# S5 outputs of two state tiles at a time, alternating between column groups of the matmul array

## Chip, cores and metric

The kernel runs on one core of a Trainium2 chip. The metric is the device time of one execution in microseconds (us). Beside the times there is one profiled execution, from which all rows of the trace come. TensorE does the matmuls (PE in the rows, PEld its weight loads), VectorE is DVE, ScalarE ACT, GpSimd POOL, SyncE SP.

## What is computed

Two layers of a decoder trunk over 512 positions and 2048 channels. Each layer projects the modulated input to four branches of 512 channels, which are gated, joined and projected back. Cut to the branch that the change is about:

```python
for l in range(DEPTH):
    h = x * (1.0 + scale) + shift
    proj = h @ w_in[l]                       # (512, 2048) @ (2048, 6144)
    y_a = gated short convolution            # a_b, a_c, a_x, a_g
    y_b = dilated attention * silu(b_g)      # q, k, v, b_g
    y_c = rglru_branch(c_x, ...) * silu(c_g)
    y_d = s5_branch(d_u, ...) * silu(d_g)
    y = concatenate([y_a, y_b, y_c, y_d]) @ w_out[l]
    x = layer_norm(ALPHA * x + (1.0 + gate) * y)

# S5: 32 groups of 16 channels, each with 64 complex diagonal states
bu = ug @ bb                                 # "drive" of the states, complex
x_re, x_im = scan(x = a * x_before + bu)     # along the positions
y = c_re . x_re - c_im . x_im + d_skip * u   # "output"
y = gelu(y); y = y * sigmoid(y @ w_glu + b_glu)
```

## The kernel before

Each layer has a branch loop of four steps (`Fori(0, CT)`), and a step makes 128 channels of every branch. The input projection is cut into 12 units of 128 channels (`UNITS`), each unit into two halves, so a step has `HALF` = 24 slots (n = 0 to 23). A slot is 24 matmuls of 128x512 in fp32r: eight with `op_hi` and eight with `op_lo` on the weights' high part, eight with `op_hi` on their low part (L915, L916, L922). All other TensorE work of a step stands behind a slot: `put(n, part)` appends a part to slot n, and TensorE does parts and slots strictly in that order. The parts that matter here:

- `s5_drive(q)`, q = 0 to 3 (slots 5, 7, 10, 13; L807): the drive of state tile q, 128 of the step's 512 complex states, into banks 2 and 3.
- `s5_output(q)` (slots 9, 12, 16, 19; L813, L814): two fp32 matmuls, with the real and the imaginary states (`s5_s[3]`, `s5_s[4]`) as moving tiles of 128x512, into the 32 partitions of bank 4 that begin at 32q, so in column group q of the array. It waits for `x_rot`, which VectorE raises at the end of `s5_out(q)`, and raises `c_done`.
- `scores(t)` (slots 9, 10, 12, 13; L835), attention scores for two heads; `p_turn(g)` (slots 16, 18, 20; L849), transposes of the probabilities, head 0 and then head 1. `p_turn(0)` waits for `p_norm` head by head. `weigh(g)` (slots 18, 20, 22; L861) multiplies probabilities and values, the two heads in two halves of the array's columns. An fp32 matmul shows as two instructions.

The outputs wait on a chain of VectorE, whose order is also written out by hand (`branch_loop`): `s5_in(q)` turns the drive, `s5_scan(q)` scans it, `s5_out(q)` turns the result back into `x_re`, `x_im` (six instructions of 128x512). All four tiles use the same five tiles `s5_s`, so `s5_out(q)` waits for `c_done` of output q - 1. Between them stand `ada` pieces (two at a time in layer 0, one in layer 1), the RG-LRU, `score_max(t)`, which waits for `scores(t)`, and `normalise(h)`, which raises `p_norm`. The part of the order around tile 2, before:

```python
score_max(3); s5_scan(2); ada(2, 1)
s5_out(2); normalise(0); ada(2, 1); normalise(1)
own(silu2(0, "c_g", gx[:, 0, :]), s.own)
dve.wait_ge(x_io.sem, 16 * (1 + (ST if l else 0)))
own(stt(y_out(2), xc, 0.5, gx[:, 0, :], MUL, MUL), s.gate_used[0])
s5_in(3); s5_scan(3); ada(2, 1); s5_out(3)
```

`own` issues an instruction and waits for its end. ScalarE (ACT) splits weights, copies units out of their banks, writes the gates' tanh and copy into `gt` and `gx` (`gate`), and copies transposed probabilities (`p_copy`) into `p_t`.

Of the kernel before, what the change touches and what calls it, by code (L numbers as in the profile page):

```python
# [31 lines left out]
ST = S // P  # L32
# [5 lines left out]
SQ = 4  # L38
# [77 lines left out]
def trunk(nc, A, out):  # L116
# [5 lines left out]
    with ExitStack() as ctx:  # L122
# [19 lines left out]
        s5_w = sb("s5_w", [P, 4, P])  # L142
# [28 lines left out]
        u_d, xc, q_t, k_t, v_t = (work[:, i, :] for i in range(5))  # L171
        u_swap = work[:, 17, :]
        s5_s = [work[:, 5 + i, :] for i in range(5)]
# [7 lines left out]
        p_t = [(work[:, 14, :], work[:, 15, :]), (q_t, k_t)]  # L181
        gx = work[:, 16:18, :]
        gt = work[:, 18:20, :]
        silu_d = work[:, 20:24, :]
        ax = xp[:, 3:3 + S]
        gel = s5_s[3]
        gate_b = work[:, 0:4, :]
        scale_acc = [ada_acc[:, 0, :], ada_acc[:, 1, :], ada_acc[:, 2, :], work[:, 20, :]]
        glu_t = work[:, 14:18, :]
# [23 lines left out]
        bank = [ctx.enter_context(nc.psum_tensor(f"bank{i}", [P, S], F32)) for i in range(8)]  # L213
# [15 lines left out]
        x_io = signal("x_io")  # L229
# [8 lines left out]
        for l in range(DEPTH):  # L238
            s, n = Layer(), f"_{l}"
# [308 lines left out]
        def _(act):  # L548
# [19 lines left out]
            for l, s in enumerate(layers):  # L568
# [26 lines left out]
                with act.Fori(0, CT) as ct:  # L595
# [10 lines left out]
                    def gate(name, i, use):  # L606
                        ps, free = unit(name)

                        act.wait_ge(s.gate_used[i].sem, s.gate_used[i].at(use, ct))
                        act.activation(gt[:, i, :], ps, ACT.Tanh, scale=0.5)  # L610
                        act.activation(gx[:, i, :], ps, ACT.Copy).then_inc(free.sem, 1)
# [9 lines left out]
                    def p_copy(g):  # L621
                        n = sum(P * (ST - kb) for kb in TURNS[g])
                        if g != 1:
                            act.wait_ge(s.pv_done.sem, s.pv_done.at(g, ct))
                        for h in range(2):
                            act.wait_ge(s.full[5 + h].sem, s.full[5 + h].at(1 + ST + g + 1, ct))
                            act.activation(p_t[h][g % 2][:, 0:n], bank[5 + h][:, 0:n], ACT.Copy).then_inc(s.p_copy.sem, 1)
# [23 lines left out]
                    for n in range(2, HALF):  # L651
                        split_hi(n, ct)
                        if n == 3:

                            act.wait_ge(s.free[4].sem, s.free[4].at(0, ct))
                            ps, free = unit("d_u")
                            act.wait_ge(s.gate_used[1].sem, s.gate_used[1].at(0, ct))
                            act.activation(u_d, ps, ACT.Copy)
                            for h in range(2):
                                swapped = act.activation(u_swap[64 * h:64 * h + 64, :], ps[64 - 64 * h:128 - 64 * h, :], ACT.Copy)  # L660
                            swapped.then_inc(free.sem, 1)
                        if n == 5:
                            act.wait_ge(s.step_end.sem, s.step_end.at(0, ct))
                            copy("c_x", xp[:, 3:3 + S])
                            rotation()
                        if n == 7:
                            copy("q", q_t, HD ** -0.5)
                        if n == 8:
                            lru()
                        if n == 9:  # L670
                            copy("k", k_t)
                        if n == 11:
                            copy("v", v_t)
                        if n == 13:
                            gate("c_g", 0, 0)
                        if n == 14:

                            act.wait_ge(s.full[7].sem, s.full[7].at(s.full[7].per, ct))
                            act.wait_ge(s.pv_done.sem, s.pv_done.at(0, ct))
                            act.activation(work[:, 10, :], bank[7][:, :], ACT.Copy).then_inc(s.free[7].sem, 1)  # L680
                        if n in (15, 16):
                            exps(n - 15)
                        if n == 15:
                            act.wait_ge(s.full[3].sem, s.full[3].at(SQ, ct))
                            gate("d_g", 1, 0)
                        if n in (18, 20, 22):
                            p_copy((n - 18) // 2)
                        if n == 17:
                            copy("a_c", va[:, 2:2 + S])
                        if n == 19:  # L690
                            copy("a_x", ax)
                        if n == 21:
                            gate("b_g", 0, 1)
                        if n == 23:
                            gate("a_g", 1, 1)
# [34 lines left out]
        def _(pe):  # L730
# [30 lines left out]
            for chunk in range(4):  # L761
                channels(layers[0], range(4 * chunk, 4 * chunk + 4))
                pe.wait_ge(pro_used.sem, KT * (chunk + 1))
                for j in range(8):
                    mm = pe.matmul(bank[7][:, j:j + 1], pro_acc[chunk % 2][:, j // 4, P * (j % 4):P * (j % 4 + 1)],
                                   ones[:, 0:1], start=True, stop=True)
                mm.then_inc(pro_sum.sem, 1)

            for l, s in enumerate(layers):
# [11 lines left out]
                with pe.Fori(0, CT) as ct:  # L781
# [25 lines left out]
                            fill(2 + i, pe.matmul(bank[2 + i][:, :], s5_w[row:row + 32, i, :], u[row:row + 32, :],  # L807
                                                  start=True, stop=True))

                    def s5_output(q):  # L810
                        pe.wait_ge(s.x_rot.sem, s.x_rot.at(q + 1, ct))
                        o = bank[4][32 * q:32 * q + 32, :]
                        pe.matmul(o, s5_w[:, 2, 32 * q:32 * q + 32], s5_s[3], start=True, stop=False)  # L813
                        mm = pe.matmul(o, s5_w[:, 3, 32 * q:32 * q + 32], s5_s[4], start=False, stop=True)  # L814
                        mm.then_inc(s.c_done.sem, 1)

                    def lru_gates():
                        pe.wait_ge(s.xc_done.sem, s.xc_done.at(1, ct))
# [70 lines left out]
                    def put(n, part, *args):  # L889
                        between[n].append(lambda: part(*args))  # L890

                    put(3, s5_turn)
                    put(6, lru_gates)
                    for q, (at_drive, at_output) in enumerate(((5, 9), (7, 12), (10, 16), (13, 19))):
                        put(at_drive, s5_drive, q)
                        put(at_output, s5_output, q)
                    for t, at in enumerate((9, 10, 12, 13)):
                        put(at, scores, t)
                    put(11, v_turn)
# [5 lines left out]
                    for n in range(HALF):  # L905
# [4 lines left out]
                        o = bank[u % 2][:, :]  # L910
                        for j in range(KH):
# [4 lines left out]
                            mm = pe.matmul(o, w_hi[:, n % NHL, w], op_lo[:, k, :], start=False, stop=False)  # L916
# [3 lines left out]
                        for j in range(KH):  # L920
                            k, w = half * KH + j, slice(P * j, P * (j + 1))
                            mm = pe.matmul(o, w_lo[:, n % NHL, w], op_hi[:, k, :], start=False, stop=k == KT - 1)  # L922
# [62 lines left out]
        def branch_loop(dve, l, s, line, own, tt, ts, stt, repeat):  # L985
# [3 lines left out]
            with dve.Fori(0, CT) as ct:  # L989
# [8 lines left out]
                def ada(*counts):  # L998

                    for _ in range(counts[l] if counts else 0):  # L1000
                        a = pieces[0]
                        pieces[0] += 1
                        chunk, k = a // KT, a % KT
                        acc, src = ada_acc[:, chunk, :], ada_in[:, a % ADA_RING, :]
                        dve.wait_ge(s.ada_in[a % ADA_RING].sem, s.ada_in[a % ADA_RING].at(16 * (a // ADA_RING + 1), ct))
                        if k:
                            dve.wait_ge(s.ada_used.sem, s.ada_used.at(a, ct))
                            stt(acc, src, cond[:, k:k + 1], acc, MUL, ADD).then_inc(s.ada_used.sem, 1)
                        else:
                            ts(acc, src, cond[:, 0:1], MUL).then_inc(s.ada_used.sem, 1)  # L1010
# [15 lines left out]
                def y_out(branch):  # L1026
                    return y_t[:, bass.ds(ct + 4 * branch, 1), :].rearrange("p o t -> p (o t)")
# [36 lines left out]
                own(stt(xc, xp[:, 0:S], col("conv_c"), xc, MUL, ADD), s.xc_done)  # L1064
                ada(2, 1)

                w_re, w_im, t_, x_re, x_im = (v.rearrange("p (a b) -> p a b", a=4) for v in s5_s)

                def turns_of(q):
                    return (rot[:, i, q, :].unsqueeze(1).to_broadcast([P, 4, TC]) for i in (1, 0))  # L1070
# [33 lines left out]
                def s5_out(q):  # L1104

                    cos, sin = turns_of(q)
                    dve.wait_ge(s.c_done.sem, s.c_done.at(q, ct))
                    own(tt(x_re, w_re, cos, MUL), s.own)
                    own(tt(t_, w_im, sin, MUL), s.own)
                    own(tt(x_re, x_re, t_, SUB), s.own)  # L1110
                    own(tt(x_im, w_im, cos, MUL), s.own)
                    own(tt(t_, w_re, sin, MUL), s.own)
                    own(tt(x_im, x_im, t_, ADD), s.x_rot)
# [24 lines left out]
                def silu2(i, use_name, dst):  # L1138

                    unit_copied(dve, s, use_name, ct)  # L1140
                    return stt(dst, gt[:, i, :], 1.0, gx[:, i, :], ADD, MUL)
# [26 lines left out]
                score_max(3)  # L1168
                s5_scan(2)
                ada(2, 1)  # L1170
                s5_out(2)
                normalise(0)
                ada(2, 1)
                normalise(1)
                own(silu2(0, "c_g", gx[:, 0, :]), s.own)

                dve.wait_ge(x_io.sem, 16 * (1 + (ST if l else 0)))
                own(stt(y_out(2), xc, 0.5, gx[:, 0, :], MUL, MUL), s.gate_used[0])
                s5_in(3)
                s5_scan(3)  # L1180
                ada(2, 1)
# [315 lines left out]
```

## Time and profile before

| | before |
|---|---|
| median of 3 runs (lowest, highest) | 1881.37 us (1880.09, 1883.77) |
| the profiled execution, its span | 1880.47 us, 1878.6 us |
| mean granted TensorE clock | 0.956 of 2.4 GHz |
| busy: TensorE, VectorE, ScalarE | 91%, 67%, 41% of the span |
| loop of layer 0, from drive 0 to drive 0 of the next step | 159.1 us |
| the same in layer 1 | 156.2 us |

In the rows a start is in us from the span's start, and the second number is how long the row's instructions took together. "x4" is four instructions in a row. A bracket at the end gives the idle time ahead of the row and what ended it; a row without one had no idle time worth showing. The granted clock is a share of full speed, 1.00 being 2.4 GHz and 0.50 being 1.2 GHz. Matmuls are pipelined, so two rows of TensorE can overlap; what a group costs is read from its start to the start of the next.

### The profile page before, as it was taken

Reading aid. Unit: us, or ns where it says so; the run is one execution under the profiler, and the core shown is the slowest. Engines: PE = TensorE matmul, PEld = TensorE weight load, DVE = VectorE, ACT = ScalarE, POOL = GpSimd, SP = SyncE. Lnnn points to the kernel's source line nnn. Section 1 sums busy time; section 2 is a strip of 40 time slices with the busy share of each in tenths; the row PEclk is TensorE's granted clock in tenths of the full one; section 3 lists DMA queues with packets and bytes.
Section 4 is the critical chain, followed back from the end, with each engine's and each line's share of the span. In section 5 each row is a group of like instructions: output and inputs, shape, how many; then the busy total and the mean of one; then the engine's idle time right before and its main releaser. Section 6 shows DMA issues by size and latency. Waiting matters only on the chain.

```text
span 1878.6 us, 23043 instructions
## 1 busy us (share of the span) xinstructions
PE 1707.7 (91%) x7527; PEld 1299.5 (69%) x7527; DVE 1253.3 (67%) x2369; ACT 778.3 (41%) x1014; POOL 232.6 (12%) x281
## 2 busy tenths in 40 slices
PE   2349999999999999899996999999999999989993
PEld 1337778767777877578875777777877777748882
DVE  5875884885687589366673585588388468544557
ACT  2135344444544445422117544545555454432120
POOL 2241111111111111000005111111111111100000
PEclk9559999999999999899997999999999999989996
DMA  7999889888978978566647878878877887737322
GB/s 265 366 324 252 202 218 227 215 210 207 240 198 209 242 195 206 151 235 198 189 129 219 201 183 189 202 183 196 205 186 191 192 201 177 177 94 253 102 89 89
DMA packets 322945, 376.07 MB, mean 200 GB/s; under 512 B 27064, under 2 KB 224032, under 8 KB 319784
## 3 DMA queue, kind: packets, MB, share of 16 engines
q1 hardware_dynamic: 294632, 272.36, 45.0%
q0 software_dynamic: 28224, 102.77, 30.1%
q14 instruction: 63, 0.52, 0.1%
q8 instruction: 26, 0.43, 0.1%
HBM read 261.81 MB, written 10.51 MB: 145 GB/s over the span
## 4 chain that ended last, share of the span: by engine, by line
PE 69%; DVE 21%; issue 4%; DMA 2%; SPq 1%; ACT 1%; POOL 0%; DVEq 0%; ACTq 0%; POOLq 0%
PE bank L915 14%; PE bank L922 14%; PE bank L916 14%; DVE work L1234 6%; PE bank L959 6%; PE bank L960 6%; PE bank L971 6%; DVE ada_acc L1242 3%; DVE work L1242 3%; PE bank L934 2%; DVE y_t L1242 1%; DVE work L1096 1%; DVE work L1095 1%; PE bank L807 1%; PE bank L861 1%
## 5 line engine op out<-in xcount | busy, mean ns | idle before, releaser
L915 PE MATMUL bank<-op_hi,w_hi 128*128 128x512 f32 x1536 | 615.7, 401 | 0.0
L916 PE MATMUL bank<-op_lo,w_hi 128*128 128x512 f32 x1536 | 601.2, 391 | 0.0
L575 ACT ACTIVATE w_hi<-raw 128x1024 fp32r<-128x1024 f32 x196 | 207.7, 1060 | 467.4 <-PE bank L916 434.8
L922 PE MATMUL bank<-op_hi,w_lo 128*128 128x512 f32 x1536 | 379.9, 389 | 4.5 <-DMA w_lo<-raw 4.4
L915 PEld LDWEIGHTS bank<-op_hi,w_hi 128*128 128x128 f32 x1536 | 289.5, 189 | 88.2 <-issue 22.2
L922 PEld LDWEIGHTS bank<-op_hi,w_lo 128*128 128x128 f32 x1536 | 288.0, 188 | 65.8 <-DMA w_lo<-raw 6.1
L916 PEld LDWEIGHTS bank<-op_lo,w_hi 128*128 128x128 f32 x1536 | 289.7, 189 | 59.8 <-issue 1.9
L527 POOL DMA_DIRECT2D w_lo<-raw x196 | 170.2, 869 | 1099.8 <-ACT w_lo L578 1075.2
L578 ACT ACTIVATE w_lo<-raw 128x1024 fp32r<-128x1024 f32 x196 | 207.1, 1057 | 125.1 <-PE bank L922 124.9
L1242 DVE SCALAR_TENSOR_TENSOR ada_acc<-ada_in,cond,ada_acc 128x512 f32<-128x512 f32 (+1 forms) x234 | 181.5, 776 | 55.3 <-DMA ada_in<-in_w_ada 34.8
L959 PE MATMUL bank<-w_hi,op_hi 128*128 128x512 f32 x512 | 200.0, 391 | 0.0
L960 PE MATMUL bank<-w_hi,op_lo 128*128 128x512 f32 x512 | 199.2, 389 | 0.0
L722 ACT ACTIVATE w_hi<-raw 128x1024 fp32r<-128x1024 f32 x60 | 63.7, 1062 | 248.2 <-PE bank L960 242.1
L1234 DVE TENSOR_TENSOR w_lo<-raw,w_hi 128x1024 fp32r<-128x1024 f32 x60 | 73.5, 1225 | 115.1 <-PE bank L971 111.5
L971 PE MATMUL bank<-w_lo,op_hi 128*128 128x512 f32 x512 | 126.5, 389 | 0.0
L1234 DVE TENSOR_TENSOR work<-bank,rot 128x512 f32<-128x512 f32 x128 | 88.5, 692 | 52.0 <-PE bank L807 47.9
L1234 DVE TENSOR_TENSOR work<-work 128x512 f32<-128x512 f32 (+2 forms) x170 | 112.5, 662 | 5.8
L959 PEld LDWEIGHTS bank<-w_hi,op_hi 128*128 128x128 f32 x512 | 96.1, 188 | 20.4 <-issue 0.5
L960 PEld LDWEIGHTS bank<-w_hi,op_lo 128*128 128x128 f32 x512 | 96.1, 188 | 20.4 <-issue 0.5
L971 PEld LDWEIGHTS bank<-w_lo,op_hi 128*128 128x128 f32 x512 | 96.1, 188 | 20.0
L1234 DVE TENSOR_TENSOR work<-work,rot 128x512 f32<-128x512 f32 x128 | 88.4, 691 | 3.6
L536 POOL TENSOR_TENSOR op_lo<-work,op_hi 128x512 fp32r<-128x512 f32 x32 | 51.4, 1618 | 307.0 <-ACT work L592 306.3
(211 smaller groups left out, 1558.7 us busy)
## 6 DMA issues: line engine op xcount, KB each, us to landing
w_lo<-raw POOLq DMA_DIRECT2D x196, 512.0 KB, 5.0
raw<-in_w_in SPq DMA_DIRECT2D x192, 512.0 KB, 4.2
ada_in<-in_w_ada SPq DMA_DIRECT2D x256, 256.0 KB, 4.4
raw<-in_w_out SPq DMA_DIRECT2D x64, 512.0 KB, 4.1
raw<-in_w_ada SPq DMA_DIRECT2D x27, 512.0 KB, 6.9
ada_in<-in_w_ada SPq DMA_DIRECT2D x18, 512.0 KB, 7.0
rot<-in_w_ada SPq DMA_DIRECT2D x10, 512.0 KB, 6.6
bias_t<-in_w_ada SPq DMA_DIRECT2D x9, 512.0 KB, 6.9
```

The lines of the kernel that those rows point to most:

```text
L527: pool.dma_start(w_lo[:, n % NHL, :], raw[:, n % NRAW, :], accum_op=ALU.add)\
L575: act.activation(w_hi[:, n % NHL, :], raw[:, n % NRAW, :], ACT.Copy).then_inc(s.hi_done.sem, 1)
L578: act.activation(w_lo[:, n % NHL, :], raw[:, n % NRAW, :], ACT.Copy, scale=-1.0)\
L722: act.activation(w_hi[:, n % NHL, :], raw[:, n % NRAW, :], ACT.Copy).then_inc(s.hi_done.sem, 1)
L915: pe.matmul(o, w_hi[:, n % NHL, w], op_hi[:, k, :], start=k == 0, stop=False)
L916: mm = pe.matmul(o, w_hi[:, n % NHL, w], op_lo[:, k, :], start=False, stop=False)
L922: mm = pe.matmul(o, w_lo[:, n % NHL, w], op_hi[:, k, :], start=False, stop=k == KT - 1)
L959: pe.matmul(o, op_hi[:, k, x_], w_hi[:, n % NHL, w_], start=k == 0, stop=False)
L960: mm = pe.matmul(o, op_lo[:, k, x_], w_hi[:, n % NHL, w_], start=False, stop=False)
L971: mm = pe.matmul(o, op_hi[:, k, x_], w_lo[:, n % NHL, w_], start=False, stop=k == KT - 1)
L1234: return dve.tensor_tensor(o, a, b, op)
L1242: return dve.scalar_tensor_tensor(o, a, sc, b, op0, op1)
```

## The change

The outputs of tiles 0 and 1 are now done together in slot 12, those of 2 and 3 in slot 19, in the order: real part of the first tile, real part of the second, imaginary part of the first, imaginary part of the second. Successive matmuls thus go to different column groups. Slots 9 and 16 have no output any more. Since two tiles' states must live at the same time, those of tile 0 go into `p_t[0]` and those of tile 2 into `gx[:, 0, :]` and `gt[:, 0, :]`; for the latter VectorE does the c_g gate and `y_out(2)` ahead of `s5_out(2)`, no longer behind `normalise(1)`. `s5_out(q)` waits for the pair before in place of the output before. ScalarE has two more waits: the first copy of probabilities waits for the first pair (it writes `p_t[0]`), and the b_g gate waits for the second pair (it writes `gx` and `gt`).

```diff
+        x_of = [p_t[0], s5_s[3:5], (gx[:, 0, :], gt[:, 0, :]), s5_s[3:5]]
...
                         if g != 1:
                             act.wait_ge(s.pv_done.sem, s.pv_done.at(g, ct))
+                        if g == 0:
+                            act.wait_ge(s.c_done.sem, s.c_done.at(2, ct))
...
                         if n == 21:
+                            act.wait_ge(s.c_done.sem, s.c_done.at(SQ, ct))
                             gate("b_g", 0, 1)
...
-                    def s5_output(q):
-                        pe.wait_ge(s.x_rot.sem, s.x_rot.at(q + 1, ct))
-                        o = bank[4][32 * q:32 * q + 32, :]
-                        pe.matmul(o, s5_w[:, 2, 32 * q:32 * q + 32], s5_s[3], start=True, stop=False)
-                        mm = pe.matmul(o, s5_w[:, 3, 32 * q:32 * q + 32], s5_s[4], start=False, stop=True)
-                        mm.then_inc(s.c_done.sem, 1)
+                    def s5_outputs(first):
+                        pe.wait_ge(s.x_rot.sem, s.x_rot.at(first + 2, ct))
+                        for i in range(2):
+                            for q in (first, first + 1):
+                                c = slice(32 * q, 32 * q + 32)
+                                mm = pe.matmul(bank[4][c, :], s5_w[:, 2 + i, c], x_of[q][i], start=i == 0, stop=i == 1)
+                                if i == 1:
+                                    mm.then_inc(s.c_done.sem, 1)
...
-                    for q, (at_drive, at_output) in enumerate(((5, 9), (7, 12), (10, 16), (13, 19))):
-                        put(at_drive, s5_drive, q)
-                        put(at_output, s5_output, q)
+                    for q, at in enumerate((5, 7, 10, 13)):
+                        put(at, s5_drive, q)
+                    put(12, s5_outputs, 0)
+                    put(19, s5_outputs, 2)
...
                     cos, sin = turns_of(q)
-                    dve.wait_ge(s.c_done.sem, s.c_done.at(q, ct))
+                    x_re, x_im = (v.rearrange("p (a b) -> p a b", a=4) for v in x_of[q])
+                    dve.wait_ge(s.c_done.sem, s.c_done.at(2 * (q // 2), ct))
...
                 ada(2, 1)
+                own(silu2(0, "c_g", gx[:, 0, :]), s.own)
+
+                dve.wait_ge(x_io.sem, 16 * (1 + (ST if l else 0)))
+                own(stt(y_out(2), xc, 0.5, gx[:, 0, :], MUL, MUL), s.gate_used[0])
                 s5_out(2)
                 normalise(0)
                 ada(2, 1)
                 normalise(1)
-                own(silu2(0, "c_g", gx[:, 0, :]), s.own)
-
-                dve.wait_ge(x_io.sem, 16 * (1 + (ST if l else 0)))
-                own(stt(y_out(2), xc, 0.5, gx[:, 0, :], MUL, MUL), s.gate_used[0])
                 s5_in(3)
```

## Rows read from the trace of the kernel before

**Rows 1.** The profile's page: busy time by engine, and its share.

```profile
PE 1707.7 (91%) x7527; PEld 1299.5 (69%) x7527; DVE 1253.3 (67%) x2369; ACT 778.3 (41%) x1014; POOL 232.6 (12%) x281
```

**Rows 2.** TensorE's waits: us in total, times, the longest.

```profile
PE bank L849 <- DVE work L1238: 4.2, 4, 1.1
...
PE bank L813 <- DVE work L1234: 2.6, 4, 0.6
```

**Rows 3.** TensorE in order of time, second step of layer 0, slots 9, 12, 16.

```profile
357.52 1.04 PE L813 MATMUL bank<-work,s_w 128*32 128x512 f32 x2
...
359.35 0.66 PE L835 MATMUL bank<-work 64*128 64x64 f32 x8
...
379.65 1.04 PE L813 MATMUL bank<-work,s_w 128*32 128x512 f32 x2 [0.65 <-DVE work L1234]
...
381.49 0.92 PE L835 MATMUL bank<-work 64*128 64x192 f32 x8
...
406.69 1.05 PE L813 MATMUL bank<-work,s_w 128*32 128x512 f32 x2
...
410.24 0.33 PE L849 MATMUL bank<-ident,ada_acc 128*128 128x128 f32 x1 [1.06 <-DVE work L1238]
```

**Rows 4.** VectorE in order of time in the same step.

```profile
332.71 1.42 DVE L1234 TENSOR_TENSOR work<-bank,rot 128x512 f32<-128x512 f32 x2 [5.58 <-PE bank L807]
...
378.90 0.69 DVE L1234 TENSOR_TENSOR work<-work 128x512 f32<-128x512 f32 x1
...
382.44 0.55 DVE L1125 CUSTOM_DVE_ANT_0 work<-bank,bias_t 128x384 f32<-128x384 f32 x1 [1.45 <-issue]
...
405.09 1.66 DVE L1238 TENSOR_SCALAR work<-work,soft 128x128 f32<-128x128 f32 x4
...
410.22 0.69 DVE L1242 SCALAR_TENSOR_TENSOR work<-work 128x512 f32<-128x512 f32 x1
...
411.82 1.42 DVE L1234 TENSOR_TENSOR work<-bank,rot 128x512 f32<-128x512 f32 x2
```

**Rows 5.** TensorE in the same step, slot 18: `weigh(0)` and what follows.

```profile
421.72 1.08 PE L861 MATMUL bank<-work 128*64 128x512 f32 x4
422.73 0.77 PE L849 MATMUL bank<-ident,work 128*128 128x128 f32 x5
```

**Rows 6.** Second step of layer 1 in order of time: VectorE and TensorE.

```profile
1236.23 0.06 DVE L1124 MEMSET spare<- 128x1 f32 x1 [1.62 <-PE bank L835]
...
1253.69 0.69 DVE L1234 TENSOR_TENSOR work<-work 128x512 f32<-128x512 f32 x1
...
1255.00 1.05 PE L813 MATMUL bank<-work,s_w 128*32 128x512 f32 x2
...
1280.71 0.49 DVE L1238 TENSOR_SCALAR work<-work,soft 128x512 f32<-128x512 f32 x1
...
1282.02 1.04 PE L813 MATMUL bank<-work,s_w 128*32 128x512 f32 x2
...
1283.36 0.49 DVE L1238 TENSOR_SCALAR work<-work,soft 128x512 f32<-128x512 f32 x1
...
1284.35 0.27 PE L849 MATMUL bank<-ident,ada_acc 128*128 128x128 f32 x1
```

**Rows 7.** Stretches: length, PE busy (instructions), granted clock, DMA share, GB/s.

```profile
1029.89:1032.39 2.50, 0.00 (x1) 1.00 1.07 211
1000.40:1003.80 3.40, 1.65 (x12) 1.00 1.03 293
1003.90:1012.90 9.00, 6.51 (x24) 0.50 0.67 172
1012.92:1014.12 1.20, 1.20 (x4) 0.50 0.58 220
783.21:788.84 5.63, 5.63 (x7) 0.50 0.00 0
...
1651.51:1655.80 4.29, 4.29 (x5) 0.50 0.00 0
```

More of the change, by code:

```diff
@@ L1065, in branch_loop @@
                 ada(2, 1)
-                w_re, w_im, t_, x_re, x_im = (v.rearrange("p (a b) -> p a b", a=4) for v in s5_s)
+                w_re, w_im, t_ = (v.rearrange("p (a b) -> p a b", a=4) for v in s5_s[0:3])
                 def turns_of(q):
```

## The prediction

> **What bounds the kernel now.** I read the profile's page first, then who waited for whom on TensorE, then the instructions in order of time. TensorE is busy 91% of the span, VectorE 67% [rows 1], so taking TensorE work out is worth something only where TensorE does not then wait for another engine. It waits in two places inside the branch loop, once in each of the four steps of layer 0, for VectorE [rows 2]: 0.65 us ahead of S5 output 1, and 1.06 us ahead of the second head's transposes of the probabilities. In layer 1 there is no such wait. The steps repeat within some 0.05 us, so one step of each layer stands for its four. The reader should see in [rows 3] and [rows 4] that VectorE finishes the sixth instruction of `s5_out(1)` at 378.90 + 0.69 = 379.59 and TensorE starts output 1 at 379.65; and that VectorE had worked without a real pause since 332.71, when it got the first drive. In layer 0 slots 6 to 12 have two engines that are both late, and VectorE is the later one.
>
> **The old and the new price of an output.** Output 1 takes from 379.65 to the scores at 381.49 = 1.84 us [rows 3], four TensorE instructions of two fp32 matmuls in one column group; the others show the same (357.52 to 359.35). Does a pair in two column groups overlap? `weigh(0)` does just this: two 128x512 fp32 matmuls, one in each half of the columns, with different moving tiles, x4 instructions as well, from 421.72 to 422.73 = 1.01 us [rows 5]. The second accumulation then adds what the second matmul of a lone output adds: 1.84 us for two against 1.01 us for one with its exit leaves some 0.85. So the new pair of outputs is 1.01 + 0.87 = 1.88 us, with 0.02 for the alternation; the lower bound is 1.84 (nothing over a lone output), the upper one, with no overlap, 2 x 1.84 = 3.68. I take 1.88, since [rows 5] is the same form but for the width of the column group. The Trainium skill (TensorE: Matmul & The Clock Gate, Part 3) says the same and puts a further tile at some 4 ns, an estimate of 1.85 us for the pair. It changes the sum by less than a microsecond.
>
> TensorE work taken out for a step: slots 9 and 16 lose 1.84 each, slots 12 and 19 gain 0.04 each: 3.6 us, 28.8 us over 8 steps. That is what the edit would give if TensorE never waited. Now each place.
>
> **Layer 0, slot 9 to 12.** TensorE is free of output 0 and comes to slot 12 1.84 us earlier. `s5_out(1)` does not get earlier: VectorE started with drive 0 (332.71), before the removed work, and found its scores ready. So the wait grows from 0.65 to 2.49 us, the pair starts at 379.65 as output 1 did, and ends 0.04 later. Gain 0, cost 0.04. VectorE then waits for `scores(2)` (1.45 us before 382.44, [rows 4]), so everything behind is 0.04 late too.
>
> **Layer 0, slot 16.** The diff also moves the c_g gate and `y_out(2)` ahead of `s5_out(2)`, because `x_of[2]` lies in gx and gt. Two instructions with their pauses: 410.22 to 411.82 = 1.60 us [rows 4]. ACT's c_g tile is there long before. Thus `normalise(0)`, which ended at 405.09 + 1.66 = 406.75, ends at 408.35, and `normalise(1)` at 411.8 in place of 410.2. TensorE transposes head 1 right behind `normalise(1)` (410.24, after a wait of 1.06, [rows 3]). It already was the late one, and taking output 2 (406.69 to 408.53) out ahead of it only makes TensorE wait: from 406.7 to 408.4, then 0.5 of transposes for head 0, then to 411.87. The end of slot 16 comes 1.60 + 0.04 us later. The gain of 1.84 is gone and the moved block costs in full. `s5_in(3)` keeps its time, since the block only went from behind to ahead; slot 19's outputs are not held up. ACT's b_g gate now waits for the pair in slot 19 (about 1 us), with its next weight split some 3 us off: nothing. Its wait ahead of the first probability copy was met in slot 12: nothing. SP's ada loads wait on pieces that VectorE does 1.6 us later; their next use is several us off: nothing. Slot 19 adds 0.04. Layer 0: 4 x (1.60 + 0.04 + 0.04) = **+6.7 us**.
>
> **Layer 1.** VectorE has half the ada pieces. It waited 1.62 us for `scores(0)` [rows 6], which now come 1.84 earlier, so `s5_out(1)` ends at 1254.38 - 1.62 = 1252.8; TensorE arrives at 1255.00 - 1.84 = 1253.2, without a wait, slack 0.4. The pair costs 1.88 for 1.84, so slot 12 is left 1.80 us earlier and VectorE, which waited for `scores(2)` and `scores(3)`, follows. Then the block: VectorE is 1.80 - 1.60 = 0.20 ahead of before; `normalise(0)` ends at 1281.20 - 0.20 = 1281.0, `normalise(1)` at 1283.85 - 0.20 = 1283.65 [rows 6]. TensorE arrives at slot 16 at 1282.02 - 1.80 = 1280.2, waits 0.8, transposes head 0 for 0.5, waits 2.1, and starts head 1 at 1283.7 in place of 1284.35. Gain 0.64, less 0.04 in slot 19: 4 x 0.60 = **-2.4 us**.
>
> The queues give 6.7 - 2.4 = +4.3 us: 1880.5 + 4.3 = 1884.8.
>
> **The clock.** TensorE now stands nearly idle in twelve stretches: 2.49 us (layer 0, slot 12), 5.1 us with 0.5 us of transposes in it (layer 0, slot 16) and 3.5 us with 0.5 in it (layer 1, slot 16). Rows on both sides [rows 7]: the 2.50 us gap at 1029.89 kept the granted clock at 1.00 (2.4 GHz). In 1000.40 to 1003.80 TensorE did short transposes, 1.65 us of 3.40, and from 1003.90 the clock was 0.50 (1.2 GHz), and still for 1.20 us of dense work. After the idle ends of the layers the dense work ran 5.63 and 4.29 us at 0.50. A fall thus costs half of 1.20 to half of 5.63: 0.6 to 2.8 us, mean of the three 1.9. Our stretches at slot 16 are emptier than 1000.40 to 1003.80 and of its length or longer: I take a fall in all 4 of layer 0 and 3 of 4 of layer 1. The 2.49 us gap equals the one that kept its clock, but the clock need not treat each alike: 2 of 4. Nine falls x 1.9 = **+17 us**; bounds 0 and 12 x 2.8 = 34. The Trainium skill (the same page, "Why this matters for your kernels") warns of just such idle gaps between bursts; the rows decide the size. A fall delays TensorE but what VectorE waits for comes late as well, so little is hidden.
>
> Sum: 1880.5 (the profiled execution; span 1878.6 and 1.9 around it) + 4.3 + 17 = **1901.8 us**. The median of the runs is 0.9 above that execution, within the noise; I say 1901.
>
> **The rivals.**
> 1. The clock holds, or falls once or twice. For it: the gaps of 0.65, 1.06 and 2.50 us kept it. Against: slot 16's are longer. Time 1884.8 to 1890.
> 2. Column groups of 32 do not overlap. For it: no row shows this width; against: [rows 5], which the other seven steps repeat. Then a pair is 3.68. Layer 0 pays 1.84 at slots 12 and 19 and 1.60 at slot 16 (+5.3 a step); layer 1 gains 1.84 on the way to slot 12 and pays it there, the block then makes normalise 1.6 late against a start of head 1 with 0.5 slack (+1.1), and slot 19 adds 1.84 (+2.9 a step): 4 x 8.2 = 33, with some falls 1920 to 1935.
> 3. Faster: VectorE has a reserve that I do not see. The pair removes a dependence of `s5_out` on the output before; if VectorE's chain came 1.84 us earlier at slot 12 and 2.5 at slot 16 in both layers, the whole 28.8 us would come through: 1852; with half of it 1866. It decides from the point at which VectorE has a pause longer than 1.84 us between drive 0 and `s5_out(1)`. Against: layer 0 has none there, and the 1.60 block stands on that chain.
> 4. Gains and losses cancel (layer 1 gains a little more, no fall): 1878 to 1884.
>
> **Chances.** My forecast 0.66 (1893 to 1908); rival 1 0.14; rival 2 0.07; rival 3 0.07; rival 4 0.06. This measurement tells about 0.2%, 3.8 us, from no change. Rival 1 at its lower end is barely above that, so I give same 0.09, faster 0.07, slower 0.84. The range takes in the forecast and rival 1: 1884 to 1908, leaving out the rest.
>
> **What would show it.** In the trace after: (a) from the first instruction of the pair to the scores 1.88 us (3.7 says rival 2); (b) in layer 0 a wait of 2.5 us ahead of the pair in slot 12, on VectorE; (c) at slot 16 waits of about 1.7 and 2.9 us in layer 0, 0.8 and 2.1 in layer 1, on VectorE; (d) a granted clock of 0.50 for 2 to 5 us behind most of these, and a mean below 0.956; (e) with (d) absent, steps of layer 0 1.7 us longer and of layer 1 0.6 shorter. I am wrong if VectorE reaches `normalise(1)` earlier than worked out, or if (d) fails.

## The result, and the profile after

| | before | after |
|---|---|---|
| median (lowest, highest) | 1881.91 us (1880.09, 1883.77) | 1903.08 us (1900.23, 1903.40) |
| ratio, 95% interval | | 1.0111 (1.0098 to 1.0124) |
| profiled execution, its span | 1880.47, 1878.6 us | 1903.40, 1901.6 us |
| mean granted clock | 0.956 | 0.942 |

The change costs 21 us. Of the executions below one, of the kernel with the later places and the outputs apart, was slow (2561.76 us at a mean granted clock of 0.649) and is not counted.

The page of the changed kernel, in its line of busy times, shows 6 us less TensorE work than [rows 1], in spite of some work done at half clock:

```profile
PE 1701.6 (89%) x7527; PEld 1311.3 (69%) x7527; DVE 1252.9 (66%) x2369; ACT 780.2 (41%) x1014; POOL 232.6 (12%) x281
```

TensorE's waits for VectorE inside the loop of the changed kernel (us in total, times, the longest). They answer to [rows 2]: the transposes' waits (L855, old L849) went from 4.2 to 28.7 us and into both layers, those ahead of an output (L819, old L813) are about as large as they were, and 5.3 us stand in a new place, ahead of a drive:

```profile
PE bank L855 <- DVE work L1246: 28.7, 16, 2.8
...
PE bank L811 <- DVE work L1242: 5.3, 4, 1.3
...
PE bank L819 <- DVE work L1242: 2.2, 2, 1.1
```

TensorE in order of time, second step of layer 0: the drive of tile 2 in slot 10, the pair in slot 12 and the scores behind it, the two heads' transposes in slot 16; then the first drives of this and of the next step. They answer to [rows 3]:

```profile
370.66 1.13 PE L811 MATMUL bank<-work,s_w 32*128 32x512 f32 x4 [1.34 <-DVE work L1242]
...
385.12 1.91 PE L819 MATMUL bank<-work,s_w 128*32 128x512 f32 x8 [1.08 <-DVE work L1242]
386.96 0.92 PE L841 MATMUL bank<-work 64*128 64x192 f32 x8
...
413.85 0.66 PE L855 MATMUL bank<-ident,work 128*128 128x128 f32 x4 [1.62 <-DVE work L1246]
417.30 0.47 PE L855 MATMUL bank<-ident,ada_acc 128*128 128x128 f32 x1 [2.79 <-DVE work L1246]
...
336.92 1.13 PE L811 MATMUL bank<-work,s_w 32*128 32x512 f32 x4
...
500.26 1.13 PE L811 MATMUL bank<-work,s_w 32*128 32x512 f32 x4
```

The pair of two outputs takes 385.12 to 386.96 = 1.84 us, as long as one output took, and so do all 16 pairs. The step from drive to drive is 163.3 us where it was 159.1. The same in the second step of layer 1, which answers to [rows 6]; there a step is 157.1 us where it was 156.2:

```profile
1227.69 1.13 PE L811 MATMUL bank<-work,s_w 32*128 32x512 f32 x4
...
1273.34 1.91 PE L819 MATMUL bank<-work,s_w 128*32 128x512 f32 x8
1275.18 0.92 PE L841 MATMUL bank<-work 64*128 64x192 f32 x8
...
1301.19 0.66 PE L855 MATMUL bank<-ident,work 128*128 128x128 f32 x4 [0.75 <-DVE work L1246]
1303.86 0.48 PE L855 MATMUL bank<-ident,ada_acc 128*128 128x128 f32 x1 [2.02 <-DVE work L1246]
...
1384.76 1.13 PE L811 MATMUL bank<-work,s_w 32*128 32x512 f32 x4
```

VectorE in the step of layer 0, the answer to [rows 4]: the moved block begins at 405.98, `s5_out(2)` at 407.57, and the last of `normalise(1)` ends at 416.75 + 0.48 = 417.23, just ahead of TensorE's 417.30.

```profile
405.98 0.68 DVE L1250 SCALAR_TENSOR_TENSOR work<-work 128x512 f32<-128x512 f32 x1
406.85 0.69 DVE L1250 SCALAR_TENSOR_TENSOR y_t<-work 128x512 f32 x1 [0.18 <-DVE work L1250]
407.57 1.42 DVE L1242 TENSOR_TENSOR work<-work,rot 128x512 f32<-128x512 f32 x2
...
416.75 0.48 DVE L1246 TENSOR_SCALAR work<-work,soft 128x512 f32<-128x512 f32 x1
```

The granted clock (columns as in [rows 7]) behind slot 16 of layer 0, behind slot 16 of layer 1, and behind slot 10 of the next step of layer 0:

```profile
415.90:423.00 7.10, 5.71 (x16) 0.52 0.40 83
...
1303.60:1307.01 3.41, 3.15 (x10) 0.51 0.73 146
...
535.62:539.03 3.41, 3.41 (x12) 0.52 0.82 157
```

From the first drive of each loop on, TensorE was busy at 0.50 for 28.5 us in layer 0 (behind slot 16 in all four steps, behind slot 10 in two) and for 12.2 us in layer 1 (behind slot 16 in all four). The kernel before has none there. By the two levels, dense work at half clock loses half its time: an estimate of 14.2 and 6.1 us, less what a later wait hides. A "fall" is from here on a change of the granted clock from 1.00 to 0.50.

One more wait bears on [rows 7], which have a gap of 2.50 us that kept its clock. It lies at the start of layer 1, ahead of the first drive, and the changed kernel has the same wait for `w_lo`, 2.61 us long. Here a fall followed:

```profile
1050.17 3.16 PE L929 MATMUL bank<-op_hi,w_lo 128*128 128x512 f32 x8 [2.61 <-DMA w_lo<-raw]
1050.95:1054.30 3.35, 3.35 (x9) 2.64 (x8) 0.00 (x0) 0.94 (x1) 0.00 (x0) 0.50 0.89 250
```

The second line is a stretch with all engines in it (PE, PEld, DVE, ACT, POOL), then the granted clock, 0.50.

### The profile page after: what moved, and what is told of

The parts are those of the page before. It is cut to its first block, busy times and chain, and to the rows that moved or that the text cites. A ratio compares the mean times of both kernels' runs of the same rounds, so it can differ in the third digit from the quotient of the medians.

```text
span 1901.6 us, 23067 instructions
## 1 busy us (share of the span) xinstructions
PE 1701.6 (89%) x7527; PEld 1311.3 (69%) x7527; DVE 1252.9 (66%) x2369; ACT 780.2 (41%) x1014; POOL 232.6 (12%) x281
## 4 chain that ended last, share of the span: by engine, by line
PE 59%; DVE 29%; issue 6%; DMA 3%; SPq 1%; ACT 1%; DVEq 0%; POOL 0%; ACTq 0%; POOLq 0%
PE bank L922 12%; PE bank L923 11%; PE bank L929 11%; DVE work L1242 10%; PE bank L967 6%; PE bank L966 6%; PE bank L978 6%; DVE ada_acc L1250 3%; DVE work L1250 3%; DVE work L1103 2%; DVE work L1102 2%; PE bank L941 2%; DVE y_t L1250 2%; DVE carry L1250 1%; DVE work L1246 1%
## 5 line engine op out<-in xcount | busy, mean ns | idle before, releaser
L922 PE MATMUL bank<-op_hi,w_hi 128*128 128x512 f32 x1536 | 627.6, 409 | 0.0
L923 PE MATMUL bank<-op_lo,w_hi 128*128 128x512 f32 x1536 | 610.3, 397 | 0.0
L922 PEld LDWEIGHTS bank<-op_hi,w_hi 128*128 128x128 f32 x1536 | 296.9, 193 | 91.0 <-issue 22.6
L923 PEld LDWEIGHTS bank<-op_lo,w_hi 128*128 128x128 f32 x1536 | 296.6, 193 | 61.9 <-issue 1.9
```

Source lines behind the costliest of these rows:

```text
L922: pe.matmul(o, w_hi[:, n % NHL, w], op_hi[:, k, :], start=k == 0, stop=False)
```

## The experiments

The kernel before ran beside each group of experiments and gave a median of 1881.1 to 1881.9 us.

**The moved block alone.** The kernel before with one move, of the c_g gate and `y_out(2)`.

```diff
                 ada(2, 1)
+                own(silu2(0, "c_g", gx[:, 0, :]), s.own)
+
+                dve.wait_ge(x_io.sem, 16 * (1 + (ST if l else 0)))
+                own(stt(y_out(2), xc, 0.5, gx[:, 0, :], MUL, MUL), s.gate_used[0])
                 s5_out(2)
                 normalise(0)
                 ada(2, 1)
                 normalise(1)
-                own(silu2(0, "c_g", gx[:, 0, :]), s.own)
-
-                dve.wait_ge(x_io.sem, 16 * (1 + (ST if l else 0)))
-                own(stt(y_out(2), xc, 0.5, gx[:, 0, :], MUL, MUL), s.gate_used[0])
```

> The kernel before with one edit: the c_g gate and y_out(2), 1.60 us of VectorE, stand ahead of s5_out(2); outputs as before. My theory (this block sits on the chain to the second head's transposes): the transposes of head 1 in slot 16 start 1.60 us later in layer 0 (4 x 1.60 = 6.4) and about 1.1 later in layer 1, where 0.5 us of slack was left (4 x 1.1 = 4.4): +11 us, with the wait in layer 0 grown from 1.06 to 2.7 us and the clock falling behind it in about half the steps (+3): 1894. Rival (the block is hidden, and the loss of the changed kernel belongs to the pairs): 1881.

1897.84 us, ratio 1.0081 (1.0064 to 1.0098). The waits of the transposes, then two first drives of layer 1:

```profile
PE bank L849 <- DVE work L1238: 14.7, 8, 2.7
...
1227.89 1.13 PE L807 MATMUL bank<-work,s_w 32*128 32x512 f32 x4
...
1385.34 1.13 PE L807 MATMUL bank<-work,s_w 32*128 32x512 f32 x4
```

The block is not hidden. The longest wait is the 2.7 us expected; in layer 1 a step is 157.45 us, 1.2 more than before. The time is 4 us above the expectation. In the profiled execution the clock fell behind slot 16 in four of four steps of layer 0, once for about 7 us, where two had been expected; from the first drives on its loops took 14.1 and 5.1 us more than before. That execution, at 1904.12 us the longest of the four, also came to its first drive 4.9 us later than the kernel before, so it tells the places and not the median.

**The first pair alone.** The kernel before with outputs 0 and 1 as a pair in slot 12. The edit is shown against the changed kernel; VectorE's order is that of before.

```diff
-        x_of = [p_t[0], s5_s[3:5], (gx[:, 0, :], gt[:, 0, :]), s5_s[3:5]]
+        x_of = [p_t[0], s5_s[3:5], s5_s[3:5], s5_s[3:5]]
...
                     put(12, s5_outputs, 0)
-                    put(19, s5_outputs, 2)
+                    put(16, s5_output, 2)
+                    put(19, s5_output, 3)
...
-                    dve.wait_ge(s.c_done.sem, s.c_done.at(2 * (q // 2), ct))
+                    dve.wait_ge(s.c_done.sem, s.c_done.at(q if q > 1 else 0, ct))
```

> The kernel before with only the first pair made: outputs 0 and 1 together in slot 12, tile 0's states in p_t[0]; outputs 2 and 3 and VectorE's order as before. My theory: in layer 0 nothing is gained, since TensorE waits for VectorE in slots 10 and 12 instead (waits of 1.3 and 1.1 us, some falls of the clock there, +0 to 3 us); in layer 1 the 1.8 us of a step come through, 4 x 1.8 = 7.2: 1874 to 1877. Rival (VectorE's chain is late in layer 1 as well, or a pair does not pay): 1881 or more.

1874.33 us, ratio 0.9960 (0.9946 to 0.9974). Waits, and two first drives of layer 1:

```profile
PE bank L810 <- DVE work L1249: 5.4, 4, 1.4
PE bank L861 <- DVE work L1253: 4.2, 4, 1.1
...
PE bank L818 <- DVE work L1249: 2.1, 2, 1.1
...
1221.81 1.13 PE L810 MATMUL bank<-work,s_w 32*128 32x512 f32 x4
...
1376.20 1.13 PE L810 MATMUL bank<-work,s_w 32*128 32x512 f32 x4
```

A step of layer 1 takes 154.39 us, 1.85 less than before: the full worth of a pair. In layer 0 the gain becomes waits ahead of the drive (L810) and the pair (L818), and the transposes wait as they did (L861, 4.2 us). So the first pair gains in layer 1 and costs next to nothing in layer 0; what makes the whole change a loss comes with the second pair and the block that is moved for it.

**The pair tile by tile.**

```diff
-                        for i in range(2):
-                            for q in (first, first + 1):
+                        for q in (first, first + 1):
+                            for i in range(2):
```

> The changed kernel with one edit: in a pair both matmuls of the first tile come ahead of both of the second, so successive matmuls stay in one column group. If the alternation is what makes them overlap: a pair takes 3.3 to 3.7 us in place of 1.9, some 1.6 us more in slots 12 and 19 of every step, all of it on TensorE's path: 16 x 1.6 = 26 us, 1925 to 1932. Rival (the array or the compiler overlaps them in any order, or the pair's time does not come from column groups): 1903.

1901.30 us, ratio 1.0103 (1.0086 to 1.0120). The rival held: a pair takes 1.85 us here, and the alternation is worth nothing. The next kernel shows why.

**A line for each matmul.** The four `matmul` lines below are L817, L818, L820 and L821; `a` is the column group of the first tile, `b` that of the second.

```diff
+                        a, b = (slice(32 * q, 32 * q + 32) for q in (first, first + 1))
+                        pe.matmul(bank[4][a, :], s5_w[:, 2, a], x_of[first][0], start=True, stop=False)
+                        mm = pe.matmul(bank[4][a, :], s5_w[:, 3, a], x_of[first][1], start=False, stop=True)
+                        mm.then_inc(s.c_done.sem, 1)
+                        pe.matmul(bank[4][b, :], s5_w[:, 2, b], x_of[first + 1][0], start=True, stop=False)
+                        mm = pe.matmul(bank[4][b, :], s5_w[:, 3, b], x_of[first + 1][1], start=False, stop=True)
+                        mm.then_inc(s.c_done.sem, 1)
```

> The changed kernel with each matmul of a pair on a line of its own, in the order first tile real, first tile imaginary, second tile real, second tile imaginary (L817, L818, L820, L821). If each column group works through its own matmuls independently of program order (what e3_by_tile points to), L820 starts within 0.1 us of L817 and L821 with L818. Rival (strict order of starts): L818 starts some 0.9 us behind L817 and L820 later still. Time as the changed kernel, 1900 to 1904.

1900.64 us in its one run. TensorE in order of time, the first pair of the second step:

```profile
382.33 0.62 PE L817 MATMUL bank<-work,s_w 128*32 128x512 f32 x1 [1.08 <-DVE work L1243]
382.35 0.62 PE L820 MATMUL bank<-work,s_w 128*32 128x512 f32 x1
382.79 0.59 PE L817 MATMUL bank<-work,s_w 128*32 128x512 f32 x1
382.80 0.59 PE L820 MATMUL bank<-work,s_w 128*32 128x512 f32 x1
383.21 0.59 PE L818 MATMUL bank<-work,s_w 128*32 128x512 f32 x1
383.23 0.59 PE L821 MATMUL bank<-work,s_w 128*32 128x512 f32 x1
```

In the program L818 stands ahead of L820; in the trace L820 starts 0.02 us behind L817 and 0.86 ahead of L818, and the other 15 pairs show the same. The compiled program keeps the order of the kernel, all instructions of the first tile ahead of those of the second, so it is not the compiler that interleaves them. In these pairs each column group works through its own matmuls, whatever stands between them.

**TensorE kept busy in slot 16.**

```diff
+FILL = ((6, 11), (3, 8))
...
                         for h in range(2):
                             if g == 0:
+                                if h == 0:
+                                    is_free(7, 1)
+                                for _ in range(FILL[l][h]):
+                                    pe.matmul(bank[7][:, :], op_hi[:, 0, 0:P], op_hi[:, 1, :], start=True, stop=True)
+                            if g == 0:
                                 pe.wait_ge(s.p_norm.sem, s.p_norm.at(h + 1, ct))
```

> The changed kernel with one addition: in slot 16, ahead of each head's first transposes, TensorE does fp32r matmuls of 128x512 into bank 7, which weigh(0) overwrites later (6 and 11 of them in layer 0, 3 and 8 in layer 1, 0.22 us each, shorter than the waits of 1.6, 2.8, 0.7 and 2.0 us that stand there). Nothing waits less. My theory (the rest of the loss is the clock): no fall to 0.50 behind slot 16, where the changed kernel has 21.6 us of busy TensorE at half clock in layer 0 and 12.2 in layer 1, half of which is lost: 1903 - 17 = 1886, 1885 to 1889. Rival (the loss is in the waits alone): 1903 or a little more.

1885.44 us, ratio 1.0023 (1.0013 to 1.0032), 17.6 below the changed kernel, by work that nobody reads. The same place as above, slot 16 of the second step, and the first drives of two steps in each layer:

```profile
410.14 0.66 PE L861 MATMUL bank<-ident,work 128*128 128x128 f32 x4 [0.28 <-DVE work L1252]
410.56 2.75 PE L853 MATMUL bank<-op_hi 128*128 128x512 f32 x11
413.59 0.33 PE L861 MATMUL bank<-ident,ada_acc 128*128 128x128 f32 x1 [0.28 <-DVE work L1252]
...
332.79 1.13 PE L812 MATMUL bank<-work,s_w 32*128 32x512 f32 x4
...
493.96 1.13 PE L812 MATMUL bank<-work,s_w 32*128 32x512 f32 x4
...
1226.86 1.13 PE L812 MATMUL bank<-work,s_w 32*128 32x512 f32 x4
...
1382.48 1.13 PE L812 MATMUL bank<-work,s_w 32*128 32x512 f32 x4
```

Head 1 is still transposed 3.45 us behind head 0 (410.14 to 413.59; 413.85 to 417.30 in the changed kernel), only with TensorE at work between them. No low clock is left behind slot 16. The step of layer 1 is now 155.62 us, 0.62 less than before the change, and that of layer 0 161.2, 2.1 more (1.6 in the third, where the clock did not fall behind slot 10 either): the queues' part by itself. In the profiled executions the two loops are 9.6 and 5.6 us shorter than in the changed kernel, 15.2 together; 2.6 of the rest stand ahead of the first drive, where the edit changes nothing.

**VectorE's normalising first.**

```diff
+                normalise(0)
+                ada(2, 1)
+                normalise(1)
                 own(silu2(0, "c_g", gx[:, 0, :]), s.own)
...
                 s5_out(2)
-                normalise(0)
-                ada(2, 1)
-                normalise(1)
```

> The changed kernel with one move: VectorE does normalise(0), the ada pieces and normalise(1) ahead of the c_g gate and s5_out(2), which the pair needs only in slot 19. My theory (the order of VectorE is what loses slot 16): the transposes no longer wait (4.4 us in layer 0, 2.8 in layer 1), no fall of the clock there; in layer 0 TensorE then waits some 2.5 us for s5_out(3) in slot 19 with a few falls behind it, so about nothing is gained against the kernel before (-1, and +4 for the clock), in layer 1 3.5 us a step (-14): 1869, 1866 to 1873. Rival (the loss is in the pairs, wherever VectorE does its part): 1895 or more.

1872.77 us, ratio 0.9954 (0.9938 to 0.9969): 30 us below the changed kernel by a change of order. The waits of the pairs:

```profile
PE bank L819 <- DVE work L1242: 13.8, 9, 2.8
```

The waits of the transposes are gone. Most of the pairs' 13.8 us are four waits of 2.8 for `s5_out(3)` in slot 19 of layer 0, and the clock fell behind three of them as well as three times behind slot 10 (22.0 us busy at 0.50 in all), which is why it ended at the upper end of the expectation.

**Drive and pairs where VectorE is ready.** This stands on top of the kernel with the normalising first. The first pair now comes later, and `s5_out(2)` no longer waits for it (`q // 3`): the states of tile 2 have a place of their own.

```diff
-                    for q, at in enumerate((5, 7, 10, 13)):
+                    for q, at in enumerate((5, 7, 11, 14)):
                         put(at, s5_drive, q)
-                    put(12, s5_outputs, 0)
-                    put(19, s5_outputs, 2)
+                    put(14, s5_outputs, 0)
+                    put(20, s5_outputs, 2)
...
-                        if n == 21:
+                        if n == 22:
                             act.wait_ge(s.c_done.sem, s.c_done.at(SQ, ct))
                             gate("b_g", 0, 1)
...
-                    dve.wait_ge(s.c_done.sem, s.c_done.at(2 * (q // 2), ct))
+                    dve.wait_ge(s.c_done.sem, s.c_done.at(2 * (q // 3), ct))
```

> The kernel of e5_norm_first with the parts put where VectorE is ready: drives of tiles 2 and 3 one slot later (11 and 14), the first pair in slot 14, the second in slot 20, the b_g gate of ACT behind slot 22's split. My theory: TensorE waits for VectorE nowhere in the loop, so the 3.6 us of a step that the pairs save come through in both layers, and layer 0 also loses its old waits of 0.65 and 1.06: 4 x 5.4 + 4 x 3.6 = 36 us, no fall of the clock: 1845, 1842 to 1850. Rival (another engine or the DMA queues become the bound when the step shrinks by 3%): 1855 to 1870, with waits of TensorE for w_lo or ACT.

1844.18 us, ratio 0.9810 (0.9796 to 0.9824). This beats both kernels. Two of the waits of TensorE that are left, neither of them between the first drive and the end of a loop, and the first drives of two steps in each layer:

```profile
PE bank L929 <- DMA w_lo<-raw: 4.0, 4, 2.5
PE bank L948 <- DVE work L1242: 2.6, 2, 1.3
...
325.19 1.13 PE L811 MATMUL bank<-work,s_w 32*128 32x512 f32 x4
...
478.61 1.13 PE L811 MATMUL bank<-work,s_w 32*128 32x512 f32 x4
...
1180.84 1.13 PE L811 MATMUL bank<-work,s_w 32*128 32x512 f32 x4
...
1333.36 1.13 PE L811 MATMUL bank<-work,s_w 32*128 32x512 f32 x4
```

153.4 us a step in layer 0 (5.7 less than before) and 152.5 in layer 1 (3.7 less); from the first drive to the end of either loop TensorE waits for nothing, and no low clock is left there.

**The same with the outputs apart.** The edit is shown against the kernel just above.

```diff
-                    put(14, s5_outputs, 0)
-                    put(20, s5_outputs, 2)
+                    for q, at in enumerate((13, 14, 19, 20)):
+                        put(at, s5_output, q)
```

> The kernel of e6_later with the outputs taken apart again: one a slot, in 13, 14, 19 and 20, each with its own wait. Nothing else differs, so it measures what the overlap alone is worth where nothing waits. My theory: 16 pairs x 1.8 us = 29 us more than e6_later: 1874. Rival (e6_later's gain comes from its order and its places): within 5 us of e6_later.

1874.84 us (median of seven executions), ratio 0.9968 (0.9958 to 0.9979), 30.7 us above the kernel with pairs. So the new order and places alone are worth 6 us and the overlap 31, or 1.9 a pair, where nothing waits.

**The drive of tile 2 a slot later.**

```diff
-                    for q, at in enumerate((5, 7, 10, 13)):
+                    for q, at in enumerate((5, 7, 11, 13)):
```

> The changed kernel with the drive of tile 2 in slot 11 in place of slot 10, nothing else. In the changed kernel TensorE waits 1.33 us for VectorE ahead of this drive in layer 0 and another 1.08 ahead of the pair in slot 12. My theory (both are one lateness of VectorE against the pair's end of s5_out(1), and only its last wait counts): the wait ahead of the drive goes, the one ahead of the pair grows to 2.4 or 2.5 us, and the pair starts as late as before, so the time stays at 1903, but for where the clock falls (the same number of falls or one or two more): 1898 to 1906. Rival (the wait ahead of the drive is a loss of its own): 4 x 1.33 = 5 us less, 1898 or below, with the wait ahead of the pair still 1.1.

1905.58 us, ratio 1.0124 (1.0107 to 1.0141). The waits in the loop:

```profile
PE bank L855 <- DVE work L1246: 28.8, 16, 2.8
...
PE bank L819 <- DVE work L1242: 9.4, 4, 2.4
```

The wait ahead of the drive is gone and the one ahead of the pair is 2.4 us in all four steps: one lateness, that of VectorE on its way to `s5_out(1)`, paid wherever TensorE first meets it. The rival would have had the time at 1898 or below. The median is 2.5 us above that of the changed kernel, but the two loops of the profiled execution, from their first drives on, take 1232.0 us for 1231.9; the difference stands ahead of the first drive of layer 0 (177.25 us for 174.06, behind a wait of 3.9 us for `w_lo`). In three of the four steps the clock fell as the pair began, behind its wait of 2.4 us.

## Why the prediction was right, point by point

The time was 1903.1 for 1901, and its terms hold in the main. In the profiled executions the loop of layer 0, from its first drive to the GLU's first matmul, grew by (802.20 - 174.06) - (783.21 - 172.32) = 17.3 us; the sum had 6.7 + 6 x 1.9 = 18.1. That of layer 1 grew by 3.5 us; the sum had -2.4 + 3 x 1.9 = 3.3. The remaining 2.2 us are mostly ahead of the first drive of layer 0, where the changed kernel waited longer for `w_lo` (2.02 us for 0.62) and a fall followed; no edit touches that stretch, and its length differs from run to run, with the first drive between 171.2 and 177.3 us.

**The price of a pair** was taken as 1.88 from the form of `weigh(0)` [rows 5]; it is 1.84. The result was right, the picture behind it was not quite. The 0.85 for the second accumulation was rounded up from 1.84 - 1.01 = 0.83, and I gave another 0.02 to the alternation, which plays no part.

**Layer 0, slots 9 to 12.** The lateness (1.34 + 1.08 = 2.42 for 2.49) and the start of the pair by VectorE came as worked out. What failed is sign (b), a wait of 2.5 us ahead of the pair: I went through the outputs and the scores on TensorE's way, and not the drive of tile 2 in slot 10, which waits until `s5_in(1)` has read the banks. This cut the predicted gap in two. It changed no time by itself, as the loops with the drive in slot 11 showed. The clock fell behind slot 10 in two steps, also a number that I had taken for slot 12; but most of the cost of these two falls was hidden, as the third step shows, which had such a fall: its pair starts 548.85 - 534.00 = 14.85 us behind the drive, in the second, without one, 385.12 - 370.66 = 14.46.

**Slot 16** came as worked out in both layers: waits of 1.62 and 2.79 us in layer 0 (I had 1.7 and 2.9), 0.75 and 2.02 in layer 1 (0.8 and 2.1). The single block and the kernel with the normalising first show the cause from both sides. Without falls behind slot 16 the step of layer 1 is 0.62 us shorter than before (forecast 0.60), that of layer 0 1.6 us longer where it had no fall at all (1.68).

**The clock** was 17 us in the sum. The filled kernel gives 17.6 back in its median, 15.2 in the loops of the profiled executions, for the eight falls behind slot 16 alone; so the agreement is good to some 2 us and no better. The count was 10 in place of 9: all four of layer 1, all four of layer 0 and two in slot 10. The mean price of 1.9 hides two sizes. Behind slot 16 of layer 0 the clock stayed low for some 7 us, of which 4.6 to 5.8 were busy (2.3 to 2.9 us lost); in layer 1 about 3.1 busy (1.5 lost); behind slot 10 1.7, largely hidden. That the mean fits is in part luck. So is the argument from the gap of 2.50 us that kept its clock: the same wait in the changed kernel, 2.61 us, did not. The Trainium skill (TensorE: Matmul & The Clock Gate, "Why this matters for your kernels") advises to avoid long idle gaps between bursts of matmuls. The trace agrees, with 40.7 us at half clock in the loops, and shows falls behind short ones too, 1.33 us ahead of the drive in slot 10.

**The rivals.** The first, a clock that holds, names the price rightly: the filled kernel, which kept the clock up behind slot 16, took 1885.44 us, within its 1884.8 to 1890. That 32-wide column groups don't overlap is refuted by 1.84 us for a pair and by 31 us between pairs and single outputs. A hidden reserve of VectorE did not show in the order as changed: TensorE waits for it at slot 16 in both layers. It can be made: the pair takes the need for `s5_out(2)` out of slot 16, and the changed kernel didn't use that. The sum that I gave as worth of the edit without waits, 28.8 us, is close to the 30.7 measured.

## What to carry to other kernels

Before making an engine's work cheaper, ask for each piece what its successor waits for: here 29 us of TensorE's work were taken out, most of it turned into waits for an engine whose order had at the same time been made worse, and the waits then cost another 15 to 18 us through the clock. When work is merged to a later place, move its producers later as well and what others wait for ahead; the same edit went from 21 us of loss to 37 of gain by order and places alone. A short wait of the matmul engine can have two prices, its own length and the low clock behind it, so count the gaps as well as the waits.

## What the runs showed of the hardware

- Two neighbouring column groups of 32, with fp32 matmuls of 128x512, ran at the same time in either order of the program: L820 started 0.02 us behind L817 and 0.86 ahead of L818, which stands between them. Alternating by hand gave nothing (1901.3 against 1903.1 us).
- A gap of 1.33 us ahead of a short drive and scores was followed by a clock of 0.50 in two of four steps of the changed kernel (first from 535.5 us) and in all four of the kernel with the pair tile by tile, whose work up to there is the same. A wait of 2.50 us for `w_lo` in [rows 7] was not followed by one, the same wait in the changed kernel (2.61 us) was. So neither the length of a gap nor the work around it settles whether the clock falls; what does stays open here.
- Matmuls that nobody reads (17 a step in layer 0, 11 in layer 1) made the kernel 17.6 us faster; the clock behind slot 16, at 0.50 in all eight steps without them, stayed at 1.00 with them.
